# Expert weights of a mixture of experts in 4 MB fetches from the ninth expert, one loop from the first expert, and another first gather

## The chip, the cores and the metric

The kernel runs on one core of one Trainium2 chip. The metric is the device time of one execution in microseconds (us), as the median of three runs. A difference under about 0.2% (2.3 us) can hardly be told from none here.

## The reference, cut to what matters

A one-layer encoder step for 256 prompt tokens and 32 sample tokens, 1024 wide: a LayerNorm, one input projection, sparse attention with an indexer, causal pooling, an output projection, a LayerNorm, then a mixture of experts and a last LayerNorm. The mixture takes most of the time. In it every token is sent to 4 of 32 experts, and each expert has 12 MB of float32 weights:

```python
for e in range(N_EXPERTS):                       # 32 experts
    gu = xt @ w1[e] + b1[e]                      # (288, 1024) @ (1024, 2048)
    gate = jnp.minimum(gu[:, :D_FF], SWIGLU_LIMIT)
    up = jnp.clip(gu[:, D_FF:], -SWIGLU_LIMIT, SWIGLU_LIMIT)
    act = (up + 1) * (gate * jax.nn.sigmoid(SWIGLU_ALPHA * gate))
    out = out + gates[:, e:e + 1] * (act @ w2[e] + b2[e])    # (288, 1024) @ (1024, 1024)
```

## The kernel before, in words

Everything up to the router is done once, in program order. Then the experts follow one after the other, and all their weights have to be read from HBM once, 403 MB.

**Weights.** `ring` in SBUF has six slots of 2 MB, so it holds exactly one expert: slots 0 to 3 are quarters of w1, slots 4 and 5 the halves of w2. Expert 0 is fetched during the stages before. After that SP fetches slot s of expert e as soon as TensorE has freed slot s of expert e - 1 (`load`, lines 455 to 459; the semaphore is `slot_free[s]`). Every partition receives 16 KB in one piece per fetch. The landing raises `w_in_slot[s]`, on which TensorE waits before it uses the slot. The last half of w2 of the last expert comes in four fetches of 512 KB, each with its own semaphore (line 471).

**One expert on TensorE** (`expert`, line 903). An expert works on a block of 64 of its tokens. (A second block for an expert with more than 64 tokens is a loop of its own, `more > 0`; with these inputs it never runs, and TensorE jumps over its code.) The steps are: the bias (line 836), 32 float32 matmuls of 512 columns for w1 (`up_products`, line 845; each is two instructions in the trace, so 64 of them, 16 for each slot), `combine` of the expert before (line 890), `gather_rows` for the next expert (line 819, needs `pick`, which VectorE makes at line 1477), the turn of the hidden values (`turn_h`, line 854), the two halves of w2 (`down_products`, line 870), and between them the transposes of the gathered rows (`turn_x`, line 828). `turn_pick` (lines 880 and 883) turns the next expert's selection matrix. The 64 tokens fill half of the array's columns, so two matmuls (g = 0, 1), for the two halves of 512 output columns, run side by side.

**The first expert.** Its tokens are gathered in another way, since the rows aren't split into bf16 parts yet: line 792 multiplies pieces of `rows`, as the stationary operand, with the selection matrix `pick0`; the 32 sample rows follow at line 806 once their selection is known, and VectorE adds the two (line 1509). After this addition VectorE makes the gates (lines 1511 to 1523, `gate_split`), the starting values of the accumulators, and splits `rows` in three bf16 parts in four instructions over all three tiles (lines 1532 to 1535, `split_ready`). Only then does it come to `pick` of expert 1.

**The order of the code.** `expert(0)` and `expert(1)` are written out, a loop runs from 2 to 30, and `expert(31, last=True)` is written out again. Each of them starts with the test for more tokens and the code of the second block.

**The tail.** After the last w2 product TensorE adds the last expert's contribution to the sums of tiles 0, 2 and 1, in this order (`start_sum`, `add_last`, lines 984 and 992). ScalarE and VectorE normalise them: ScalarE starts with tile 2's sum (line 1213), then takes the root for tile 0 (line 1006), on which VectorE's `centre(0)` waits (line 1615) before `centre(1)` begins (line 1607). GpSimd has one addition at the end.

```python
def load(e, s):
    src = w1_part(col(e), s) if s < 4 else w2_v[col(e), s - 4]
    sp.wait_ge(slot_free[s], e)
    sp.dma_start(ring[:, s, :], src.rearrange("e p n -> p (e n)")).then_inc(w_in_slot[s], 16)
```

## Time and profile before

| | |
|---|---|
| median of 3 runs | 1136.07 us (1135.74 to 1136.48) |
| the profiled execution's own time | 1135.52 us |
| its span in the trace | 1133.7 us |
| TensorE matmul busy | 1058.4 us, 93% |
| VectorE, ScalarE, GpSimd busy | 397.8, 195.4, 15.4 us |
| read from HBM | 420.11 MB |
| chain that ended last | DMA 50%, TensorE 40%, VectorE 8% |
| fetches of 2 MB into `ring` | 191, median 22.0 us from issue to landing |

The span is cut into 40 slices of 28.3 us in the page of the profile. Up to the seventh the data rate is below 330 GB/s, from the ninth to the thirty-eighth it is 427 to 430 GB/s. Busy shares are averages: both TensorE and the DMA engines look full, and which of them sets the time has to be read from what waits for what in each stretch.

### The profile page before, as it was taken

To read this page: it belongs to the slowest core of one execution; us is meant where nothing else is said; L and a number is where in the kernel's file an instruction comes from. 1 tells how busy PE (TensorE), PEld (TensorE's weight loads), DVE (VectorE), ACT (ScalarE), POOL (GpSimd) and SP (SyncE) were. 2 spreads that over 40 slices of the span, in tenths; PEclk is the share of its full clock that TensorE was granted. 3 is DMA by queue.
4 is the path that set the end of the run, shared out by engine and by line. 5 is a ranking of instruction groups with operands and counts; after the bars stand their busy time and mean duration, and the time that the engine had idled before them with its cause. 6 is when DMAs were issued, how large, how long until landed. Compare 5 with 4: busy or idle time off the path is not lost.

```text
span 1133.7 us, 13776 instructions
## 1 busy us (share of the span) xinstructions
PE 1058.4 (93%) x5318; PEld 438.3 (39%) x5319; DVE 397.8 (35%) x682; ACT 195.4 (17%) x439; POOL 15.4 (1%) x26
## 2 busy tenths in 40 slices
PE   8989999999999999999999999999999999999986
PEld 7765465333333333333333333333333333333331
DVE  7682357322333332222222222222222222222215
ACT  3334110111111111111111111111111111111113
POOL 1003000000000000000000000000000000000000
PEclk9999897999999999999999999999999999999988
DMA  9750333999999999999999999999999999999991
GB/s 324 265 223 1 126 136 156 380 427 427 429 430 427 429 430 427 429 429 428 429 429 428 429 428 428 429 428 428 429 428 429 429 427 430 429 427 430 429 380 42
DMA packets 37633, 421.91 MB, mean 372 GB/s; under 512 B 6333, under 2 KB 6973, under 8 KB 13066
## 3 DMA queue, kind: packets, MB, share of 16 engines
q1 hardware_dynamic: 37418, 420.93, 88.5%
q10 hardware_dynamic: 192, 0.66, 0.2%
q8 instruction: 16, 0.26, 0.1%
q14 instruction: 7, 0.06, 0.0%
HBM read 420.11 MB, written 1.46 MB: 372 GB/s over the span
## 4 chain that ended last, share of the span: by engine, by line
DMA 50%; PE 40%; DVE 8%; issue 1%; ACT 1%; DVEq 0%; SPq 0%; ACTq 0%
DMA ring<-in_w_dram 49%; PE ps L845 18%; PE ps L870 6%; PE ps L576 4%; PE ps L693 3%; PE ps L890 1%; DVE area L1563 1%; PE ps L555 1%; PE ps L792 1%; DVE area L1554 1%; DVE area L1557 1%; DVE area L1550 1%; PE ps L640 1%; PE ps L828 1%; DVE area L1551 1%
## 5 line engine op out<-in xcount | busy, mean ns | idle before, releaser
L845 PE MATMUL ps<-ring,area 128*64 128x512 f32 x2048 | 453.7, 597 | 26.6 <-DMA ring<-in_w_dram 26.6
L845 PEld LDWEIGHTS ps<-ring,area 128*64 128x64 f32 x2048 | 142.5, 138 | 320.4 <-issue 254.6
L870 PE MATMUL ps<-ring,area 128*64 128x512 f32 x1024 | 231.9, 595 | 0.0
L1550 DVE TENSOR_SCALAR area<-ps 128x512 f32<-128x512 f32 x32 | 22.1, 691 | 382.3 <-PE ps L845 382.3
L1563 DVE TENSOR_TENSOR area<-area,ps 128x1024 f32<-128x1024 f32 (+1 forms) x96 | 116.4, 1214 | 51.9 <-PE ps L890 51.9
L870 PEld LDWEIGHTS ps<-ring,area 128*64 128x64 f32 x1024 | 69.7, 136 | 124.8 <-issue 122.3
L1177 ACT ACTIVATE area<-area 128x512 f32<-128x512 f32 x32 | 20.1, 630 | 492.8 <-DVE area L1550 492.8
L1542 DVE SCALAR_TENSOR_TENSOR y_sb<-ps,gcol,y_sb 64x512 fp32r<-64x512 f32 x62 | 46.5, 751 | 98.4 <-ACT y_sb L1149 98.0
L890 PE MATMUL ps<-y_sb,giveT 128*128 128x512 f32 x192 | 69.4, 443 | 11.9 <-DVE area L1563 11.9
L819 PE MATMUL ps<-area 128*64 128x512 bf16 x558 | 66.1, 382 | 2.2 <-DVE area L1477 2.2
L1149 ACT ACTIVATE y_sb<-ps,gcol 64x512 fp32r<-64x512 f32 x62 | 42.4, 683 | 92.4 <-PE ps L870 91.7
L576 PE MATMUL ps<-tokT,area 128*128 128x288 f32 (+1 forms) x224 | 56.8, 414 | 0.0
L576 PEld LDWEIGHTS ps<-tokT,area 128*128 128x128 f32 (+1 forms) x224 | 42.2, 190 | 13.5 <-issue 0.9
L890 PEld LDWEIGHTS ps<-y_sb,giveT 128*128 128x128 f32 x192 | 29.1, 191 | 43.1 <-issue 25.1
L1196 ACT COPY area<-ps 128x512 f32<-128x512 f32 x31 | 18.2, 587 | 154.4 <-PE ps L828 154.4
L819 PEld LDWEIGHTS ps<-area 128*64 128x64 bf16 x558 | 28.9, 109 | 35.9 <-issue 11.0
L1483 DVE CAST sel<-same_exp 96x64 bf16 (+1 forms) x32 | 6.1, 192 | 82.3 <-PE ps L870 82.3
L854 PE MATMUL ps<-ident,area 128*128 128x128 f32 x128 | 23.8, 309 | 8.3 <-DVE area L1557 8.3
L828 PEld LDWEIGHTS ps<-ident,tokT 128*128 128x128 f32 x124 | 17.3, 209 | 25.2 <-issue 25.2
L854 PEld LDWEIGHTS ps<-ident,area 128*128 128x128 f32 x128 | 17.8, 208 | 23.6 <-DVE area L1557 21.3
L836 PE MATMUL ps<-area,sel 96*64 96x512 bf16 x128 | 20.8, 406 | 5.5 <-issue 4.6
L1477 DVE TENSOR_TENSOR area<-iota_slot,kv_rows 128x384 bf16<-128x384 f32 (+2 forms) x33 | 18.0, 546 | 22.2 <-issue 22.1
(231 smaller groups left out, 627.0 us busy)
## 6 DMA issues: line engine op xcount, KB each, us to landing
ring<-in_w_dram SPq DMA_DIRECT2D x191, 2048.0 KB, 22.0
area<-in_w_o_dram SPq DMA_DIRECT2D x1, 4096.0 KB, 13.4
area<-in_w_in_dram SPq DMA_DIRECT2D x1, 2560.0 KB, 16.2
area<-in_w_in_dram SPq DMA_DIRECT2D x1, 2336.0 KB, 9.2
area<-in_w_in_dram SPq DMA_DIRECT2D x1, 2048.0 KB, 20.4
ring<-in_w_dram SPq DMA_DIRECT2D x4, 512.0 KB, 19.8
lnb<-in_ln_g_dram SPq DMA_DIRECT2D x3, 512.0 KB, 10.4
lnb<-in_ln_b_dram SPq DMA_DIRECT2D x3, 512.0 KB, 11.7
```

The lines of the kernel that those rows point to most:

```text
L576: last = mm(ps[0:w, proj_bank(i), 0:TOK], w_in_sb[chunk][:, j, c0:c0 + w], tokT[:, j, :], start=(j == 0), stop=(j == KT - 1))
L693: last = mm(dst, mixed[:, k, t0:t0 + n], w_o_sb[:, k, half * 512:(half + 1) * 512], start=(start and k == ks[0]), stop=(stop and k == ks[-1]))
L819: last = mm(ps[g * BLK:(g + 1) * BLK, 2, :], one[:, t, 0, :], rows_b[:, t, part, g * 512:(g + 1) * 512], start=(t == 0 and part == 0), sto ...
L828: last = tr(ps[:, 2, c * P:(c + 1) * P], gx[:, c:512:4], ident[:, :])
L845: last = mm(ps_gu[g * BLK:(g + 1) * BLK, c, :], x[:, spot(k), :], w[:, a:a + 512], start=False, stop=(k == KT - 1))
L854: last = tr(dst[:, c * P:(c + 1) * P], h_sb[:, c:512:4], ident[:, :])
L870: last = mm(ps_y[g * BLK:(g + 1) * BLK, :], hT[:, c, h, :], w2_t[:, h, c, g * 512:(g + 1) * 512], start=False, stop=(h == 1 and c == 3))
L890: last = mm(dst[:, g, :], giveT[:, t * P:(t + 1) * P], y_sb[:, g * 512:(g + 1) * 512], start=True, stop=True)
L1149: nc.scalar.activation(y_sb[0:BLK, g * 512:(g + 1) * 512], ps_y[r, :], ACT.Copy, scale=gcol[r, :]).then_inc(done, 1)
L1542: ins = v.scalar_tensor_tensor(y_sb[BLK:P, g * 512:(g + 1) * 512], ps_y[r, :], gcol[r, :], y_sb[0:BLK, g * 512:(g + 1) * 512].bitcast(F32) ...
L1550: v.tensor_scalar(g_sb, ps_gu[:, 0, :], LIMIT, None, ALU.min).then_inc(gate, 1)
L1563: v.tensor_tensor(acc, acc, src[0:n, :, :], ALU.add).then_inc(done, 1)
```

## The change

1. **Fetches.** Experts 1 to 8 are fetched as before, now in a loop. From expert 9 (`FIRST_WIDE`) to expert 30 SP fetches pairs of slots, 4 MB each with 32 KB in one piece for every partition (`load_pair`), and waits for both slots of a pair to be free. Expert 31 is fetched by slots of 2 MB, the last one too.
2. **The signal.** A pair raises only `w_in_slot[s]`. GpSimd waits for it and raises `w_in_slot[s + 1]`.
3. **Layout.** For w2 to lie in 32 KB pieces, partition p now holds rows 8p to 8p + 7. So that the hidden values come out in that order, the w1 product reads its moving operand in groups of 4 columns, every other group (`half_of`): g = 0 takes columns 0 to 3, 8 to 11, ..., g = 1 the others. The bias is read in the same way.
4. **First gather.** `pick0` is now the stationary operand and `rows` the moving one: six matmuls of 512 columns, then a copy by ScalarE, `turn_x`, and a copy to `xT`. The addition on VectorE is gone. `turn_pick` for expert 0, with its wait for `gate_split`, moves ahead of the first w1 product.
5. **Split.** The split of `rows` is done tile by tile, in 12 instructions instead of 4.
6. **Loop.** The loop runs from expert 0 to 30, and the test for more tokens of the next expert (`more_tokens(e + 1)`) stands at its end.
7. **Tail.** The last sums are made in the order of tiles 0, 1, 2.

```diff
-        w2_v = w2[0].rearrange("e (h p c) n -> e h p (c n)", h=2, c=4)
+        w2_v = w2[0].rearrange("e (p h c) n -> e h p (c n)", h=2, c=4)
+        w2_whole = w2[0].rearrange("e (p q) n -> e p (q n)", q=KT)
@@ SP
+            def load_pair(e, s):
+
+                src = w1_v[col(e), s // 2] if s < 4 else w2_whole[col(e)]
+                sp.wait_ge(slot_free[s], e)
+                sp.wait_ge(slot_free[s + 1], e)
+                sp.dma_start(ring[:, s:s + 2, :], src.rearrange("e p n -> p (e n)")).then_inc(w_in_slot[s], 16)
+
+            with sp.Fori(1, FIRST_WIDE) as e:
                 for s in range(NSLOT):
                     load(e, s)
-            for s in range(NSLOT - 1):
+            with sp.Fori(FIRST_WIDE, NE - 1) as e:
+                for s in range(0, NSLOT, 2):
+                    load_pair(e, s)
+            for s in range(NSLOT):
                 load(NE - 1, s)
-            sp.wait_ge(slot_free[5], NE - 1)
-            for c in range(4):
-                sp.dma_start(w2_t[:, 1, c, :], w2_v[NE - 1, 1, :, c * D:(c + 1) * D]).then_inc(tail_in[c], 16)
@@ GpSimd
+            with pool.Fori(FIRST_WIDE, NE - 1) as e:
+                for s in range(0, NSLOT, 2):
+                    pool.wait_ge(w_in_slot[s], 16 * (e + 1))
+                    pool.sem_inc(w_in_slot[s + 1], 16)
@@ TensorE
+            def gather_first(t, stop):
+
+                for g in range(2):
+                    last = mm(ps[g * BLK:(g + 1) * BLK, 2, :], pick0[:, t, 0, :], rows[:, t, g * 512:(g + 1) * 512],
+                              start=(t == 0), stop=stop)
+                return last
...
+            keep_warm(4)
             pe.wait_ge(pick_ready, 1)
+            gather_first(2, True).then_inc(x_first, 1)
...
+            def half_of(w, c, g):
+
+                return w[:, c * F:(c + 1) * F].rearrange("p (m g q) -> p m g q", g=2, q=4)[:, :, g, :]
...
-                            last = mm(ps_gu[g * BLK:(g + 1) * BLK, c, :], x[:, spot(k), :], w[:, a:a + 512],
+                            last = mm(ps_gu[g * BLK:(g + 1) * BLK, c, :], x[:, spot(k), :], half_of(w, c, g),
...
+            keep_warm(4)
+            turn_x(x_first_sb, 1, x_gathered)
+            pe.wait_ge(gate_split, 1)
+            turn_pick(pick, ps_g, slice(0, 1), giveT_done)
...
-                    for t in (2, 1):
+                    for t in (1, 2):
...
-            expert(0)
-            expert(1)
-            with pe.Fori(2, NE - 1) as e:
+            more_tokens(0)
+            with pe.Fori(0, NE - 1) as e:
                 expert(e)
+                more_tokens(e + 1)
@@ VectorE
-            dve.wait_ge(x_first_sb, 1)
-            dve.wait_ge(x_gathered, 1)
-            v.tensor_tensor(xT, xT, ps[:, 3, :].rearrange("p (k s) -> p k s", k=KT), ALU.add).then_inc(xT_ready, 1)
...
+            dve.wait_ge(x_gathered, 1)
+            for t in range(NT):
+                link(v.tensor_copy(rows_b[:, t, 0, :], rows[:, t, :]))
...
```

SyncE's queue, its loop of fetches. Before, six fetches of a slot (128x4096 float32, 2 MB) for an expert:

```order
L459 ISA [waits slot_free0]
L459 DMA ring<-in_w_dram 128x4096
L459 ISA [waits slot_free1]
L459 DMA ring<-in_w_dram 128x4096
L459 ISA [waits slot_free2]
L459 DMA ring<-in_w_dram 128x4096
```

With the change, from expert 9 to 30:

```order
L467 ISA [waits slot_free1,slot_free0]
L467 DMA ring<-in_w_dram 128x8192
L467 ISA [waits slot_free3,slot_free2]
L467 DMA ring<-in_w_dram 128x8192
L467 ISA [waits slot_free5,slot_free4]
L467 DMA ring<-in_w_dram 128x8192
```

Half as many fetches stand in the queue, each twice as large and behind two waits.

TensorE's stream at the last expert. Before, between the end of the loop (L976) and the last expert's bias (L836) stood the code of the second block:

```order
L976 COMPARE_AND_BRANCH
L904 TENSOR_LOAD blocks_i
L904 ISA x2
L905 COMPARE_AND_BRANCH
L906 TENSOR_LOAD blocks_i
L906 ISA x2
L907 UNCONDITIONAL_BRANCH
L812 ISA
L819 MATMUL ps<-area,tokT 64x512 x18
```

With the change that code is inside the loop, and the last expert's products (L847, L855) follow right behind the loop's end (L989):

```order
L920 COMPARE_AND_BRANCH
L918 UNCONDITIONAL_BRANCH
L989 REGISTER_ALU
L989 COMPARE_AND_BRANCH
L847 MATMUL ps<-area,sel 64x512 x4
L855 MATMUL ps<-ring,area 64x512 x32
L897 MATMUL ps<-y_sb,giveT 128x512 x4
```

So the jump over the second block's code is no longer the last thing between the loop and the last expert.

TensorE's stream before the first expert. Before, the gather (L792, L806: sixteen and eight matmuls of 64 columns) ran up to the test for more tokens:

```order
L792 MATMUL ps<-area,rows 128x64 x8
L555 MATMUL ps<-ident 128x128 x2
L806 MATMUL ps<-area,rows 128x64 x8
L904 TENSOR_LOAD blocks_i
L904 ISA x2
L905 COMPARE_AND_BRANCH
```

With the change:

```order
L565 MATMUL ps<-ident 128x128 x4
L803 MATMUL ps<-rows,area 64x512 x2
L565 MATMUL ps<-ident 128x128 x4
L836 MATMUL ps<-ident,tokT 128x128 x4
L887 MATMUL ps<-ident_b,area 128x128 x3
L890 MATMUL ps<-gate_b,area 128x3 x3
L917 TENSOR_LOAD blocks_i
```

The gather is shorter, and the transposes (L836) and `turn_pick` (L887, L890) now stand between it and the test.

## Rows read from the trace of the kernel before

**Rows 1.** Stretches: from:to, us, busy us (x) PE PEld DVE ACT POOL, clock, DMA, GB/s

```profile
198.00:227.00 29.00, 25.87 (x136) 9.71 (x138) 10.49 (x13) 4.34 (x9) 0.00 (x0) 1.00 0.93 381
312.00:600.00 288.00, 275.44 (x1408) 99.81 (x1408) 85.66 (x112) 43.78 (x91) 0.00 (x0) 1.00 1.01 428
1086.00:1092.00 6.00, 5.18 (x16) 1.88 (x18) 0.00 (x0) 0.00 (x0) 0.00 (x0) 0.50 1.02 429
```

**Rows 2.** Chain that ended last: start us, us, what

```profile
423.40 24.82 DMA ring<-in_w_dram
...
1035.57 3.68 PE ps L845 x16
1039.41 25.47 DMA ring<-in_w_dram
```

**Rows 3.** Timeline before the first expert's products: start us, us, engine, line, operation, idle

```profile
180.07 0.69 DVE L1509 TENSOR_TENSOR area<-area,ps 128x512 f32<-128x512 f32 x1 [5.87 <-PE ps L806]
180.81 1.06 PE L836 MATMUL ps<-area,sel 96*64 96x512 bf16 x4 [0.85 <-DVE area L1509]
183.15 0.27 DVE L1523 TENSOR_TENSOR gate_b<-kv_rows,gate_b 128x99 bf16<-128x99 f32 x1
```

**Rows 4.** DMA queues, PE's code queue q8, in 175:182 and in 1082:1104

```profile
q8 instruction: 2, 0.03, 1.8%
...
q8 instruction: 2, 0.03, 0.6%
```

**Rows 5.** Timeline, first expert's turn from up to down products

```profile
197.24 0.70 PE L890 MATMUL ps<-y_sb,giveT 128*128 128x512 f32 x2
200.16 2.13 PE L819 MATMUL ps<-area 128*64 128x512 bf16 x18 [2.22 <-DVE area L1477]
204.91 3.60 PE L870 MATMUL ps<-ring,area 128*64 128x512 f32 x16
```

**Rows 6.** DMA packets and data queue, 66:74 (w_o, 4 KB runs), then 250:1080

```profile
DMA packets 807, 3.31 MB, mean 414 GB/s; under 512 B 0, under 2 KB 0, under 8 KB 806
q1 hardware_dynamic: 806, 3.30, 101.1%
...
DMA packets 24420, 355.60 MB, mean 428 GB/s; under 512 B 2716, under 2 KB 2716, under 8 KB 2716
q1 hardware_dynamic: 24419, 355.59, 100.6%
```

**Rows 7.** Timeline of TensorE, experts 29 and 30, then the last

```profile
1039.15 0.73 PE L890 MATMUL ps<-y_sb,giveT 128*128 128x512 f32 x2
1053.22 10.47 PE L845 MATMUL ps<-ring,area 128*64 128x512 f32 x48
1064.93 3.65 PE L845 MATMUL ps<-ring,area 128*64 128x512 f32 x16 [1.24 <-DMA ring<-in_w_dram]
...
1086.82 1.06 PE L836 MATMUL ps<-area,sel 96*64 96x512 bf16 x4 [4.63 <-issue]
1087.65 16.37 PE L845 MATMUL ps<-ring,area 128*64 128x512 f32 x64
```

**Rows 8.** Table load of ScalarE at line 1177: duration min/median/max ns, start

```profile
L1177 ACT ACT_TABLE_LOAD  x1: 1283/1283/1283, 176.4 to 176.4; - x1
```

**Rows 9.** Weight loads: min/median/max ns, first and last start us

```profile
L792 PEld LDWEIGHTS ps<-area,rows x32: 308/329/331, 167.4 to 174.9; 128*128 128x128 f32 x32
...
L762 PEld LDWEIGHTS ps<-w_router_sb,tokT x48: 106/192/192, 157.5 to 166.6; 128*128 128x128 f32 x32, 128*32 128x32 f32 x16
```

**Rows 10.** Timeline of the tail: last sums and what follows

```profile
1120.42 1.05 PE L992 MATMUL ps<-tokT 64*32 64x512 f32 x4
1121.52 1.01 ACT L1213 ACTIVATE area<-ps 32x1024 f32<-32x1024 f32 x1 [5.04 <-PE ps L992]
1122.98 0.16 DVE L1615 RECIPROCAL rstd<-std 128x1 f32<-128x1 f32 x1 [1.28 <-ACT std L1006]
1124.49 1.30 DVE L1607 BATCH_NORM_STATS2 stats<-ps 128x6 f32<-128x512 f32 x2 [1.35 <-PE ps L992]
```

More of the change, by code:

```diff
@@ L309, in encoder_kernel @@
         acc_done = [sem(f"acc_done{t}") for t in range(NT)]
-        tail_in = [sem(f"tail_in{c}") for c in range(4)]
         last_give = sem("last_give")
@@ L789, in _ @@
             pe.wait_ge(pick_first, 1)
[L790 to L803 removed]
+            def gather_first(t, stop):
[3 more added lines that the diff above has]
+                return last
+            gather_first(0, False)
+            gather_first(1, False)
+            pe.wait_ge(gates_ready, 2)
+            for u in range(NT):
+                mm(ps[:, 5, 0:NE], before[:, :] if u == 2 else ones_b[:, :], chosen_b[:, u, :],
+                   start=(u == 0), stop=(u == 2))
+            for u in range(NT):
+                total = mm(ps[:, 5, NE:2 * NE], ones_b[:, :], chosen_b[:, u, :],
+                           start=(u == 0), stop=(u == 2))
+            total.then_inc(prefix_ps, 1)
+            keep_warm(4)
             pe.wait_ge(pick_ready, 1)
[L805 to L808 removed]
+            gather_first(2, True).then_inc(x_first, 1)
             def gather_rows(one, ready, want, done, e):
                 pe.wait_ge(ready, want)
[L813 to L815 removed]
                 for t in range(NT):
@@ L927, in expert @@
                             pe.wait_ge(x_acc_done[t], b + 1)
+            def expert(e, last=False):
                 pe.wait_ge(xT_ready, e + 1)
@@ L952, in expert @@
                     return
-                if isinstance(e, int) and e == 0:
-                    pe.wait_ge(gate_split, 1)
-                    turn_pick(pick, ps_g, slice(0, 1), giveT_done)
                 pe.wait_ge(y_ready, e + 1)
@@ L1152, in _, with more_tokens @@
             act.wait_ge(x_first, 1)
-            copy(xT, ps_x).then_inc(x_first_sb, 1)
+            copy(gx, ps[:, 2, :]).then_inc(x_first_sb, 1)
+            act.wait_ge(x_gathered, 1)
+            copy(xT, ps_x).then_inc(xT_ready, 1)
             act.wait_ge(blocks_ready, 1)
-            def expert(e, last=False):
+            def more_tokens(e):
                 more = act.value_load(blocks_i[0:1, 0, col(e)], min_val=0, max_val=LAST_BLK - 1)
@@ L1175, in expert @@
                         nc.scalar.activation(x_y, ps_y, ACT.Copy, scale=x_gcol[:, :]).then_inc(x_y_ready, 1)
+            def expert(e, last=False):
                 act.wait_ge(gate_ready, e + 1)
@@ L1204, in expert @@
                 gated_high(y_high)
-            expert(0)
-            expert(1)
-            with act.Fori(2, NE - 1) as e:
+            more_tokens(0)
+            with act.Fori(0, NE - 1) as e:
                 expert(e)
+                more_tokens(e + 1)
             expert(NE - 1, last=True)
@@ L1565, in _, with more_tokens @@
             dve.wait_ge(blocks_ready, 1)
-            def expert(e, last=False):
+            def more_tokens(e):
                 more = dve.value_load(blocks_i[0:1, 0, col(e)], min_val=0, max_val=LAST_BLK - 1)
@@ L1576, in expert @@
                             accumulate(t, x_comb_done[t], b + 1, x_acc_done[t])
+            def expert(e, last=False):
                 if not last:
@@ L1581, in expert @@
                 if last:
-                    for t in (0, 2, 1):
+                    for t in range(NT):
                         accumulate(t, comb_done[t], NE, acc_done[t], src=ps_sum[t])
@@ L1593, in expert @@
                 gated_low(e)
-            expert(0)
-            expert(1)
-            with dve.Fori(2, NE - 1) as e:
+            more_tokens(0)
+            with dve.Fori(0, NE - 1) as e:
                 expert(e)
+                more_tokens(e + 1)
             expert(NE - 1, last=True)
```

45 lines of the change are left out of this document (9 added, 36 removed).

## The prediction

> **What bounds the kernel now.** I read the stretches first, then the chain of waits, then the timeline at the places where the chain changes hands. In the stretches the reader is to see that from the middle of the first experts on the DMA engines are full, at 428 GB/s, while TensorE is busy 275 of 288 us [rows 1]: both look like the bound. The chain decides it. From 423 us on its pieces are a fetch of 25 us and 3.7 us of TensorE, over and over [rows 2]; TensorE waits at the last slot of w1 in each expert, and one period is 1064.93 - 1035.57 = 29.36 us [rows 2, 7]. A slot is 2.10 MB, at 428 GB/s 4.9 us, so a fetch that lands after 25 us has spent 20 of them behind others: the queue of transfers is the bound, not the latency of one. TensorE alone would need 14.07 us from the end of the w1 products to the next ones (1039.15 to 1053.22 [rows 7]) and 64 x 0.218 = 14.0 us for these (48 instructions in 10.47 us [rows 7]), some 28.0 us. So the end of the kernel is the time at which the stream of refills starts, plus 31 experts' transfers, plus what TensorE does after it has lost touch with the stream at the end.
>
> That last part is not short. The last expert's bias starts only after 4.63 us in which TensorE waits for nothing the profile shows, and its w1 products take 16.37 us, for 14.0 elsewhere [rows 7]; the granted clock is 0.50, the 1.2 GHz level, in the stretch behind that idle time [rows 1]. Two packets of 16 KB on TensorE's code queue fall in this stretch [rows 4], while of 24420 packets in 250 to 1080 us all but one are data [rows 6]: I read the 4.63 us as code that had to be fetched, since it stands beyond the loop and beyond the jump over the second block. The last weights are there before they are needed, so the four small fetches at the end hide nothing.
>
> **The change, part by part**, each against the profiled execution's own 1135.52 us, which is 0.55 us under the median.
>
> *Larger packets.* The fetch of w_o in 4 KB packets shows 1.011 x 16 engines x 8 us / 806 = 160.5 ns a packet; in the long stretch, without the 2716 signals, it is 1.006 x 16 x 830 / 21704 = 615.5 ns for 16 KB [rows 6]. A line through the two has 8.8 ns fixed and 37.0 ns per KB of 1000 bytes. A 32 KB packet then takes 1222 instead of 1231 ns, 0.71% less. What counts is the transfers from expert 9 to w1 of expert 30, 21.7 x 29.36 = 636 us: a gain of 4.5 us. Bounds: 0, if the engines cut the run into 16 KB anyway or the difference isn't fixed; 9, if the fixed part is twice my two-point value.
> By the Trainium skill (DMA: Bandwidth & Descriptors, Why small descriptors are slow) a packet has a fixed overhead of about 3 cycles; at the 850 MHz that the same page gives for the fabric this is 3.5 ns where the trace has 8.8, and an estimate by that page would be a gain of 1.8 us instead of 4.5, the whole sum 2.7 us higher.
>
> *Pairs.* SP now waits for two slots. When slot 3 of expert 9 was asked for, at 423.40 us, it landed 24.82 us later [rows 2], with 4.9 of its own: some 18 us of other transfers stood ahead. Waiting for the second slot costs 16 x 0.218 = 3.5 us in w1, and somewhat more in w2, so from expert 9 on the queue never runs dry: 0. GpSimd's forwarding is needed only 3.5 us after the landing, and GpSimd has nothing else to do: 0. But TensorE gets slots 2 and 3 at one time and has 7.1 us to do after the landing instead of 3.65. Its cycle from landing to landing becomes 7.1 + 14.07 + 7.0 = 28.2 us, still under 29.1, so nothing is lost in the loop; at the end, where TensorE alone sets the pace, it is 3.5 us later.
>
> *The last expert's code.* It now stands directly behind the loop's end, which has been run 30 times, so the first part needs no fetch and the next can come during 14.0 us of products. I take the 4.63 us away, and with them the slow clock. TensorE would start these products 7.1 + 14.07 = 21.2 us after the landing in expert 30 (before: 1087.65 - 1064.93 = 22.7), and need 14.0 instead of 16.4: 35.2 instead of 39.1, with the pairs 3.9 us earlier. The last slot of w1 lands 29.4 us after that landing and is needed 31.6 after, so no wait comes back. Bounds: 7.0 worse if the code is still fetched.
>
> *Tail order.* Before, ScalarE began with tile 2 at 1121.52, VectorE had tile 0's root at 1122.98, and `centre(1)` started at 1124.49 with its sum [rows 10]. Now tile 2 comes last, when tile 1 did, at about 1124.45. ScalarE starts 3.0 us later, the root is ready 1.46 + 0.2 us after that, and `centre(1)` starts at 1126.2: 1.7 us lost. Nothing covers it. The four small fetches go at no cost, since the slot has landed well before the w2 product.
>
> *Start.* The old gather's weight loads go by 0.24 us each (32 in 7.5 us [rows 9]), 48 in all; the six new matmuls cost 0.43 us each. VectorE, which sat idle 5.87 us before the addition [rows 3], goes on at once; its gate work (180.76 to 183.42 [rows 3]) ends at 174.2 - 2.0 + 2.7 = 174.9 us, the 2.0 because the counts' matmuls come after four short instead of sixteen slow instructions. TensorE turns `pick` until 175.5. Then comes the jump over the second block. Two code packets lie in 175 to 182 us [rows 4]: this jump misses as the last expert's did. With 4.6 us for it the products start at 180.2 instead of 180.8 [rows 3]: -0.5 us. Bounds: -5.3 if the code is there, +1.0 if the fetch is a bit slower than that.
>
> *First turn.* Between the w1 and w2 products of expert 0 TensorE waited 2.22 us for `pick`, and went from 197.24 to 204.91 [rows 5]. VectorE is now 8.5 us earlier with the gates, far more than the 12 instructions in place of 4 can add. The w2 product starts about 3 us earlier, and the refill of slot 4 with it. In this stretch the stream carried 381 instead of 428 GB/s, 3.2 us lost in 29 [rows 1]; I give 2.0 back, bounds 0 and 3.2.
>
> *The strided read.* 0, with the rival below. *The table load* in ScalarE's loop, 1.28 us [rows 8], lies in the 14.0 us of products in which ScalarE has nothing to do; if it came later it would delay the sigmoid by as much, inside TensorE's 1 us of slack. *The loop from 0* and the register arithmetic: 0, the matmul queue covers them.
>
> Sum: -4.5 - 3.9 + 1.7 - 0.5 - 2.0 = -9.2 us, 1126.3 for the profiled execution, **1126.8** on the scale of the median.
>
> **Rivals.**
> *A, the strided read makes TensorE the bound (slower).* For it: where a weight load reads one float of every four (line 792) it takes 329 ns, where it reads in a row (line 762) 192 [rows 9], 137 ns for 128 columns. The new moving read skips a group of four after each group, 128 times per instruction. If a skip costs what a lone float did, it is 0.137 us for each of 32 side-by-side pairs, 4.4 us per expert. The cycle is then 28.0 + 4.4 = 32.4, over 29.36, and 30 of them take 972 us where 906 pass now from the first bias to the last (180.81 to 1086.82 [rows 3, 7]); with 2.0 for the last products and 1.7 for the tail that is 1136.1 + 69.7 = 1206 us. It decides from 0.26 of this price on (28.2 + 1.16 = 29.36). Against it: groups of four floats are not single ones.
> On this the Trainium skill (SBUF — State Buffer, Specifications (TRN2)) says that lines are 16 bytes and that only reads with fewer than two hits in a line lose bandwidth. Four floats fill a line, and by that rule A doesn't happen; the two weight loads agree with it.
> *B, no larger packets.* The transfers are cut as before: -4.7, 1131.4. For it: no packet over 16 KB is in the trace. Against it: every run up to 16 KB came as one packet [rows 6].
> *C, the last expert's code is fetched all the same.* +7.0: -2.2, 1133.9. B and C together: +2.3, 1138.4.
> *D, the first jump finds its code,* or the stream starts earlier for another reason: -14.0, 1122.1.
>
> **How the numbers follow.** Forecast 0.38, B 0.20, C 0.16, B and C 0.07, D 0.10, A 0.09. Faster by over 0.2% (2.3 us, about what a measurement can tell): forecast, B, D and the better part of C, 0.06: 0.74. Within it: the rest of C and half of B with C: 0.13. Slower: A and the rest: 0.13. The range runs from just under D, 1121.5, to just over B with C, 1139; A is left out.
>
> **What would show it.** Data packets of 32 KB and over 430 GB/s from 420 us on; a period of 29.1 us with TensorE waiting at slot 2 for about 1 us, not at slots 2 and 3; no idle time of 4 us before the last bias and 14.0 us for the last w1 products; `centre(1)` 1.7 us later behind the last w2 product than before; no wait of line 827 for `pick` in expert 0. Wrong is the forecast if 48 instructions of line 855 in a row take more than 10.5 us, if the rate stays at 428, or if SP's queue of fetches runs empty after expert 9.

## The result, and the profile after

| | before | after |
|---|---|---|
| median | 1136.07 us | 1128.09 us (1127.28 to 1129.7) |
| ratio to before, 95% interval | | 0.9921 [0.9908, 0.9934] |
| the profiled execution's own time | 1135.52 us | 1127.28 us |
| its span | 1133.7 us | 1125.5 us |
| ScalarE busy | 195.4 us | 234.3 us (31 table loads, 39.8 us) |

The change makes the kernel 0.8% faster, 8.0 us by the medians and 8.2 us by the two profiled executions. The forecast was 1126.8 us, in a range from 1121.5 to 1139.

The stretches after (from:to, us, busy us (x) of PE PEld DVE ACT POOL, clock, DMA, GB/s), for [rows 1]:

```profile
198.00:227.00 29.00, 28.44 (x154) 10.66 (x152) 9.42 (x13) 5.93 (x11) 0.00 (x0) 1.00 1.00 425
312.00:600.00 288.00, 275.42 (x1397) 100.31 (x1397) 83.72 (x110) 55.54 (x99) 0.00 (x0) 0.99 1.01 431
```

Behind the first expert the stream of weights carries 425 instead of 381 GB/s, from expert 9 on 432 instead of 428 (431 over the second stretch, which begins before that). The chain that ended last, for [rows 2]:

```profile
1027.79 7.11 PE ps L855 x32
1035.10 21.79 DMA ring<-in_w_dram
1056.93 7.11 PE ps L855 x32
1078.21 13.76 PE ps L855 x64
```

It is still a fetch and TensorE in turn, with 7.1 us of products behind each landing instead of 3.7, and one period is 1056.93 - 1027.79 = 29.14 us (29.36 before). Behind expert 30 no fetch stands in it. TensorE's timeline from the first turn and from the end, for [rows 5, 7] (start us, us, engine, line, operation, idle time before it):

```profile
180.37 16.55 PE L855 MATMUL ps<-ring,area 128*64 128x512 f32 x64
...
197.51 2.13 PE L827 MATMUL ps<-area 128*64 128x512 bf16 x18
...
201.86 3.60 PE L877 MATMUL ps<-ring,area 128*64 128x512 f32 x16
...
1056.93 7.09 PE L855 MATMUL ps<-ring,area 128*64 128x512 f32 x32 [0.99 <-DMA ring<-in_w_dram]
...
1077.57 0.64 PE L847 MATMUL ps<-area,sel 96*64 96x512 bf16 x4
1078.04 13.90 PE L855 MATMUL ps<-ring,area 128*64 128x512 f32 x64
1091.88 1.20 PE L897 MATMUL ps<-y_sb,giveT 128*128 128x512 f32 x4
1094.96 0.72 PE L864 MATMUL ps<-ident,area 128*128 128x128 f32 x4 [1.88 <-DVE area L1577]
...
1096.59 8.73 PE L877 MATMUL ps<-ring,area 128*64 128x512 f32 x32
```

The first products of the kernel before, beside the first of these lines:

```profile
181.67 15.38 PE L845 MATMUL ps<-ring,area 128*64 128x512 f32 x64
```

They now start 1.30 us earlier but take 1.17 us longer. Three things are gone: the wait for `pick` in expert 0, the 4.63 us ahead of the last bias, and the slow last w1 products (13.90 instead of 16.37 us). One thing is new: the last w2 products. Their 32 instructions ran from 1108.66 to 1115.62 us before, in 6.96 us; now they take 8.66 (the next instruction of TensorE, the first sum, starts at 1105.25). The granted clock, the third number from the end in these stretches, says why:

```profile
1093.00:1096.60 3.60, 1.51 (x11) 0.95 (x12) 3.22 (x5) 3.06 (x7) 0.00 (x0) 1.00 0.28 114
1096.70:1100.00 3.30, 3.30 (x12) 0.81 (x10) 1.82 (x2) 0.00 (x0) 0.00 (x0) 0.50 0.00 0
```

The clock was at 0.50, the 1.2 GHz level, for some 3.4 us. Ahead of that TensorE had worked 1.51 of 3.6 us, since it waited 1.88 us for the gated hidden values.

Cut at the points where the chain changes hands, the 8.2 us lie as follows:

| stretch (us) | before | after | change | forecast |
|---|---|---|---|---|
| from the start to the first refill asked for | 186.79 | 186.80 | 0.0 | -0.5 |
| from there to the landing of slot 3 (with 2) in expert 9 | 261.43 | 258.13 | -3.3 | -2.0 |
| from there to the same in expert 30 | 616.71 | 612.00 | -4.7 | -4.5 |
| landing to the end of the last w1 products | 39.02 | 34.95 | -4.1 | -3.9 |
| the turn between w1 and w2 | 4.71 | 4.71 | 0.0 | 0 |
| last w2 products | 6.96 | 8.66 | +1.7 | 0 |
| from there to the end of the span | 18.08 | 20.25 | +2.2 | +1.7 |
| sum | | | -8.2 | -9.2 |

The landings are at 423.40 + 24.82 = 448.22 and at 1064.93 us before [rows 2, 7], and at 444.93 and 1056.93 us after.

### The profile page after: what moved, and what is told of

Its sections match the earlier page's. It is cut to its first block, busy times and chain, and to the rows that moved or that the text cites. A ratio compares the mean times of both kernels' runs of the same rounds, so it can differ in the third digit from the quotient of the medians.

```text
span 1125.5 us, 13844 instructions
## 1 busy us (share of the span) xinstructions
PE 1054.6 (94%) x5298; PEld 437.2 (39%) x5299; DVE 395.4 (35%) x689; ACT 234.3 (21%) x470; POOL 15.4 (1%) x26
## 4 chain that ended last, share of the span: by engine, by line
PE 49%; DMA 41%; DVE 7%; issue 1%; ACT 1%; SPq 0%; DVEq 0%; ACTq 0%
DMA ring<-in_w_dram 41%; PE ps L855 27%; PE ps L877 7%; PE ps L586 4%; PE ps L703 3%; PE ps L897 1%; DVE area L1583 1%; PE ps L565 1%; DVE area L1574 1%; DVE area L1577 1%; DVE area L1570 1%; PE ps L847 1%; PE ps L836 1%; DVE area L1571 1%; PE ps L650 1%
## 5 line engine op out<-in xcount | busy, mean ns | idle before, releaser
L855 PE MATMUL ps<-ring,area 128*64 128x512 f32 x2048 | 453.7, 597 | 22.9 <-DMA ring<-in_w_dram 22.9
L855 PEld LDWEIGHTS ps<-ring,area 128*64 128x64 f32 x2048 | 149.7, 138 | 309.6 <-issue 257.3
L877 PEld LDWEIGHTS ps<-ring,area 128*64 128x64 f32 x1024 | 70.1, 137 | 126.1 <-issue 123.7
L1198 ACT ACT_TABLE_LOAD x31 | 39.8, 1283 | 1.0 <-issue 0.5
L836 PEld LDWEIGHTS ps<-ident,tokT 128*128 128x128 f32 x128 | 17.8, 209 | 25.2 <-issue 25.2
L1213 ACT COPY tokT<-ps 128x512 f32<-128x512 f32 x31 | 18.1, 585 | 42.4 <-PE ps L827 42.4
```

The lines of the kernel that those rows point to most:

```text
L855: last = mm(ps_gu[g * BLK:(g + 1) * BLK, c, :], x[:, spot(k), :], half_of(w, c, g), start=False, stop=(k == KT - 1))
L877: last = mm(ps_y[g * BLK:(g + 1) * BLK, :], hT[:, c, h, :], w2_t[:, h, c, g * 512:(g + 1) * 512], start=False, stop=(h == 1 and c == 3))
L1198: nc.scalar.activation(sig_sb, g_sb, ACT.Sigmoid, scale=SWIGLU_ALPHA).then_inc(sig_ready, 1)
```

## The experiments

Each group was compared with the kernel before on its own chip: 1137.30 us for no pairs, pairs of 16 KB runs, the old order of the last sums and the small matmuls; 1136.13 for the code moved, the code put back, the late pick and no first test; 1136.97 for the two shifts, one float of four and the combined version. The start of the program differs between executions by up to 3.0 us (the first refill goes out at 186.6 to 189.6 us in kernels with the same start), which is as much as some of the effects; where a profile shows the stretch, the stretch decides.

### Packets and pairs

**No pairs.** All fetches by slots, as in `with sp.Fori(1, NE - 1)`, and no loop on GpSimd:

```diff
-            with sp.Fori(1, FIRST_WIDE) as e:
+            with sp.Fori(1, NE - 1) as e:
                 for s in range(NSLOT):
                     load(e, s)
-            with sp.Fori(FIRST_WIDE, NE - 1) as e:
-                for s in range(0, NSLOT, 2):
-                    load_pair(e, s)
```

> The changed kernel with every fetch one slot of 2 MB in 16 KB packets, no pairs, no forwarding on GpSimd. If the 32 KB packets raised the rate, the period goes back from 29.14 to 29.36 us (21.7 of them: +4.7), but TensorE gets the slots one by one, which brings the last expert's products up to 3.5 us closer to the landing in expert 30, less 1.2 us that they then wait for their last slot of w1: in sum 1130.5 us. If the packets did nothing and the better rate has another cause, it is 1125.8 us: the period stays and the phase of the pairs is won back.

Measured: 1128.57 us, ratio 0.9925 [0.9911, 0.9938].

**Pairs of 16 KB runs.**

```diff
+        w1_quarters = w1[0].rearrange("e (h a p c) n -> e h p a (c n)", h=2, a=2, c=2)
+        w2_halves = w2[0].rearrange("e (a p c) n -> e p a (c n)", a=2, c=4)
-                src = w1_v[col(e), s // 2] if s < 4 else w2_whole[col(e)]
+                src = w1_quarters[col(e), s // 2] if s < 4 else w2_halves[col(e)]
...
-                sp.dma_start(ring[:, s:s + 2, :], src.rearrange("e p n -> p (e n)")).then_inc(w_in_slot[s], 16)
+                sp.dma_start(ring[:, s:s + 2, :], src.rearrange("e p a n -> p (e a) n")).then_inc(w_in_slot[s], 16)
```

> The pairs of 4 MB stay, with the same waits, signals and number of fetches, but each partition gets them in two runs of 16 KB from two places of the row range (the rows of w1 and w2 then lie in other partitions than the products assume, so the output is another; the amount of work is the same). If the packet's size is what counts, the packets take 615 ns each and the period is 29.36 us: 21.7 x 0.22 = +4.7, 1132.8 us. If it is that a fetch is larger, or that there are fewer signals, it stays at 1128.1 us.

Measured: 1132.90 us, ratio 0.9957 [0.9943, 0.9970]. The packets of 430 to 1050 us: first the changed kernel, then this one (count and rate, then the data queue with packets, MB and share of 16 engines):

```profile
DMA packets 9194, 267.72 MB, mean 432 GB/s; under 512 B 1024, under 2 KB 1024, under 8 KB 1024
q1 hardware_dynamic: 9194, 267.72, 100.3%
```

```profile
DMA packets 17221, 265.64 MB, mean 428 GB/s; under 512 B 1008, under 2 KB 1008, under 8 KB 1008
q1 hardware_dynamic: 17221, 265.64, 100.6%
```

The same 4 MB fetches, waits and signals with 16 KB runs are back at 428 GB/s. Their period, from the timeline:

```profile
1034.89 7.09 PE L856 MATMUL ps<-ring,area 128*64 128x512 f32 x32 [1.22 <-DMA ring<-in_w_dram]
...
1064.25 7.09 PE L856 MATMUL ps<-ring,area 128*64 128x512 f32 x32 [1.22 <-DMA ring<-in_w_dram]
```

It is 29.36 us. So it is the packet's size that counts, and neither the size of a fetch nor the number of signals. The kernel without pairs has the same period, 1091.15 - 1061.80 = 29.35 us:

```profile
1061.80 3.65 PE L847 MATMUL ps<-ring,area 128*64 128x512 f32 x16 [1.22 <-DMA ring<-in_w_dram]
...
1091.15 3.65 PE L847 MATMUL ps<-ring,area 128*64 128x512 f32 x16 [1.20 <-DMA ring<-in_w_dram]
1094.73 1.20 PE L889 MATMUL ps<-y_sb,giveT 128*128 128x512 f32 x4
```

Its landing in expert 30 is 4.9 us later than in the changed kernel, and from it to the end of the last w1 products pass 1094.73 - 1061.80 = 32.9 us instead of 34.95: the pairs cost 2.0 us at the end, with the 1.2 us wait for the last slot that I had expected. That it came out at 1128.6 and not at 1130.5 us has one more cause: its clock does not fall in the last w2 products (7.03 us), which saves 1.7. So the larger packets with their pairs bring 2.9 us where the clock stays up, and in this pair of kernels the clock gives most of that back.

### The last expert's code

**The kernel before with the code moved**, on TensorE alone:

```diff
-            def expert(e, last=False):
+            def more_tokens(e):
...
...
+            def expert(e, last=False):
                 pe.wait_ge(xT_ready, e + 1)
...
+            more_tokens(0)
             expert(0)
+            more_tokens(1)
             expert(1)
+            more_tokens(2)
             with pe.Fori(2, NE - 1) as e:
                 expert(e)
+                more_tokens(e + 1)
```

> The kernel before, with one edit on TensorE alone: the test for more tokens and the second block's code stand at the end of an expert instead of at its head, so the last expert's products follow right behind the loop. If the 4.63 us and the slow clock behind them are code that has to be fetched, they go: the last up products end 31.7 us after the landing in expert 30, plus 1.2 us that they then wait for their last slot, where it was 39.0: 6.1 us less, 1130.0 us (1131.7 if the clock then falls in the last w2 products, as in the changed kernel). If they come from the register reads of the test, which stay, it is 1136.1 us.

Measured: 1133.36 us, ratio 0.9974 [0.9965, 0.9983]. At the last expert the idle time and the slow clock are gone:

```profile
1068.06 3.65 PE L845 MATMUL ps<-ring,area 128*64 128x512 f32 x16 [1.23 <-DMA ring<-in_w_dram]
...
1085.26 0.62 PE L836 MATMUL ps<-area,sel 96*64 96x512 bf16 x4
...
1097.43 3.65 PE L845 MATMUL ps<-ring,area 128*64 128x512 f32 x16 [1.25 <-DMA ring<-in_w_dram]
```

From the landing to the end of the w1 products it takes 32.9 instead of 39.0 us, the 6.1 that I had worked out. The test's register reads are still there, so they were not the cause. But only half of it reaches the result. Most of the rest went at the start of expert 3:

```profile
274.58 1.06 PE L836 MATMUL ps<-area,sel 96*64 96x512 bf16 x4 [4.88 <-issue]
```

The idle time has moved: 4.88 us of it, with the clock at 0.50 behind it, and the landing in expert 30 is 3.1 us later than in the kernel before [rows 7], 0.5 of it from a later start (the first refill goes out at 187.32 us). 3.1 - 6.1 = -3.0 us, which is 1133.1.

**The code put back in the changed kernel.**

```diff
-            more_tokens(0)
             with pe.Fori(0, NE - 1) as e:
+                more_tokens(e)
                 expert(e)
-                more_tokens(e + 1)
+            more_tokens(NE - 1)
```

> The changed kernel with the opposite edit on TensorE alone: the test and the second block's code stand at the head of the loop and once more between the loop and the last expert. Code theory: the idle time of 4 to 5 us and the half clock come back before and in the last w1 products: +7.0, less 1.7 if the clock then does not fall in the w2 products: 1133.4 to 1135.1 us. Rival, that pairs or larger packets shortened this stretch: 1128.1 us.

Measured: 1128.29 us, ratio 0.9930 [0.9917, 0.9943]. TensorE at the last expert, and its code queue between 1076 and 1092 us:

```profile
1078.67 0.64 PE L847 MATMUL ps<-area,sel 96*64 96x512 bf16 x4
```

```profile
q8 instruction: 1, 0.02, 0.4%
```

This was a clear miss. The second block's code stands between the loop and the last expert again, TensorE jumps over it, and there is no idle time. One code packet comes in these 16 us (two in the kernel before, none in the changed one), but TensorE doesn't wait for it: it starts at 1080.7 us, while the products run. In each of the four idle times of 4.6 to 5.5 us of this document a packet on the code queue starts 1.7 to 2.4 us after TensorE has stopped (at 1084.1 us in the kernel before, where TensorE stops at 1082.2), and TensorE goes on 1.6 to 2.2 us after it has ended. So code that must be fetched is still the best reading of the 4.63 us, though no run takes the packet away alone. But "behind a jump" isn't the condition. A new theory: it depends on where in memory the loop's end and the last expert lie, relative to the pieces in which code is fetched. Two kernels tried it, with nothing else changed than the number of small matmuls at the very start, where TensorE waits for its input.

```diff
             pe.wait_ge(ident_ready, 1)
-            keep_warm(12)
+            keep_warm(20)
```

> The kernel before with eight small matmuls more at its very start, where TensorE waits anyway: nothing else than that all of its later code lies a little further on. The run with the code put back showed no idle time at the last expert though the jump was there, so what counts may be where the loop and the last expert lie against the pieces in which code is fetched. If the shift brings the loop's end and the last expert's code to such a place, the 4.63 us and the slow clock go as in the run with the code moved: 1133.4 us or, with the 6.1 us worked out there, 1130.0. If what counts is the order of the code alone, it stays at 1136.1 us.

Measured: 1132.87 us, ratio 0.9965 [0.9953, 0.9977]. TensorE:

```profile
1066.76 3.65 PE L845 MATMUL ps<-ring,area 128*64 128x512 f32 x16 [1.24 <-DMA ring<-in_w_dram]
...
1083.96 0.62 PE L836 MATMUL ps<-area,sel 96*64 96x512 bf16 x4
```

Eight matmuls more at the start of the old kernel, and the 4.63 us at its end are gone; from the landing to the end of the w1 products it takes 32.9 us, as with the code moved. So the order of the code alone doesn't make the idle time. (1.6 of the 6.1 us went again since here the clock falls at the last w2 products: 8.34 us instead of 6.96, and 0.2 in the turn before them. Another 1.8 went because the landing in expert 30 is later, 1.0 of it from a later start of the refills.) The shift also made a new idle time of 1.84 us, and not right at a jump: TensorE stops in the middle of the w1 products of expert 2, 2.3 us after it began that expert's bias. A code packet starts at 243.9 us, 0.7 before the stop.

```profile
246.43 12.61 PE L845 MATMUL ps<-ring,area 128*64 128x512 f32 x57 [1.84 <-issue]
```

The other one, with `keep_warm(4)` in the kernel with the code put back:

> The run with the code put back (second block ahead of the last expert), with eight small matmuls fewer at the very start: its code lies a little nearer. If the place against the pieces of code counts, the idle time of 4 to 5 us before the last bias and the half clock behind it come back: 1133.4 to 1135.1 us. If the order of the code or the loop from expert 0 is what counts, no idle time and 1128.3 us.

Measured: 1125.58 us, ratio 0.9893 [0.9877, 0.9909]. No idle time came back at the last expert, so the condition stays unknown, and this one shift neither shows nor refutes that the place in memory counts: three kernels that have the jump there (this one and the two before it) don't wait, and the kernel before does. The shift worked at another place, at the first jump:

```profile
179.13 0.66 PE L847 MATMUL ps<-area,sel 96*64 96x512 bf16 x4 [1.42 <-issue]
```

Here TensorE waits 1.42 us. The same kernel without the shift, and then the changed kernel:

```profile
181.11 1.06 PE L847 MATMUL ps<-area,sel 96*64 96x512 bf16 x4 [4.61 <-issue]
```

```profile
177.19 0.39 PE L847 MATMUL ps<-area,sel 96*64 96x512 bf16 x1 [1.32 <-issue]
179.93 1.06 PE L847 MATMUL ps<-area,sel 96*64 96x512 bf16 x3 [2.35 <-issue]
```

The intervals of the two kernels with the code put back are apart: 0.9930 against 0.9893, some 3 us for eight small matmuls. In the profiles the first refill goes out at 187.73 us without the shift and at 185.10 with it.

### The start and the first turn

**No first test.** `more_tokens(0)` left out on TensorE: a second block of expert 0 wouldn't be computed.

> The changed kernel without the test for more tokens and the second block of expert 0 on TensorE (with these inputs it never runs): no jump stands ahead of the first products. If the 1.32 and 2.35 us of idle time around the first bias are the jump's missing code, the first w1 products start at 177.6 instead of 180.4 us and the whole stream 2.8 us earlier: 1125.3 us. If the code has to be fetched whether there is a jump or not, 1128.1 us.

Measured: 1126.02 us, ratio 0.9905 [0.9891, 0.9919].

```profile
175.98 13.93 PE L855 MATMUL ps<-ring,area 128*64 128x512 f32 x64
...
209.17 1.07 PE L847 MATMUL ps<-area,sel 96*64 96x512 bf16 x4 [5.53 <-issue]
```

The first idle time goes, and with it the slow clock that made the first 64 products take 16.55 us in the changed kernel: the first refill goes out at 179.80 us, 7.0 earlier. But the first jump is now the one at the end of expert 0, and it costs 5.53 us with the clock at 0.50 behind it. In 198 to 227 us the stream carries 325 GB/s, and most of the lead is lost: the landing in expert 30 is at 1056.48 us, 0.45 earlier, and the profiled execution is 0.5 us faster. That the idle time goes with the first jump holds for this pair of kernels and is no rule: with the code moved it came at expert 3, behind several jumps.

**A late pick.** In the changed kernel, on VectorE:

```diff
+                for _ in range(8 if t == 2 else 0):
+                    link(v.tensor_tensor(rows_b[:, t, 2, :], rows[:, t, :], rows_b[:, t, 1, :], ALU.subtract))
                 v.tensor_tensor(rows_b[:, t, 2, :], rows[:, t, :], rows_b[:, t, 1, :], ALU.subtract).then_inc(split_ready, 1)
```

> The changed kernel with eight repeats of the last instruction of the split on VectorE (1.23 us each, 9.8 in all), so that pick of expert 1 is ready at 200.3 us as before and not at 190.5. If the first turn is where 3.3 us of the stream came from, TensorE waits 2.2 us again between the w1 and w2 products of expert 0, the stretch of 29 us behind it carries some 380 instead of 428 GB/s, and the time is 1131.2 us. If the stream would have caught up anyway (the queue refills later), it is 1128.1 us.

Measured: 1130.73 us, ratio 0.9952 [0.9939, 0.9965].

```profile
200.56 2.13 PE L827 MATMUL ps<-area 128*64 128x512 bf16 x18 [3.05 <-DVE area L1498]
...
1060.46 7.09 PE L855 MATMUL ps<-ring,area 128*64 128x512 f32 x32 [0.99 <-DMA ring<-in_w_dram]
```

TensorE waits 3.05 us. Its first w2 product starts at 205.31 us, 3.45 later than in the changed kernel, and 860 us later the landing in expert 30 is 1060.46 - 1056.93 = 3.5 us later: nothing in between made up for it. This shows what an early `pick` is worth; which part of the change makes it early, the new gather or the split tile by tile, no run tells apart.

### The tail and the clock

**The old order of the last sums:** `(2, 1)` again on TensorE and `(0, 2, 1)` on VectorE.

> The changed kernel with the old order of the last sums (tiles 0, 2, 1) on TensorE and VectorE. My theory: the sum of tile 1 on VectorE starts 1.55 us earlier behind the last w2 product (8.87 instead of 10.42 us), and the end comes as much earlier: 1126.5 us. The rival, that the last store sets the end whatever the order: within 0.3 us of 1128.1.

Measured: 1126.56 us, ratio 0.9900 [0.9885, 0.9916]. The tail from the first of the last sums on, and the last two stores, of this kernel and of the changed one:

```profile
1107.99 1.98 PE L998 MATMUL ps<-area,ident 128*128 128x512 f32 x4
...
1116.86 1.30 DVE L1632 BATCH_NORM_STATS2 stats<-ps 128x6 f32<-128x512 f32 x2 [1.34 <-PE ps L1006]
...
1122.49 0.34 SPq L478 DMA_DIRECT2D out_dram<-area  x1
1123.67 0.35 ACTq L1256 DMA_DIRECT2D out_dram<-area  x1
```

```profile
1105.25 1.98 PE L998 MATMUL ps<-area,ident 128*128 128x512 f32 x4
...
1115.67 1.28 DVE L1632 BATCH_NORM_STATS2 stats<-ps 128x6 f32<-128x512 f32 x2
...
1121.28 0.34 SPq L478 DMA_DIRECT2D out_dram<-area  x1
1122.46 0.35 ACTq L1256 DMA_DIRECT2D out_dram<-area  x1
```

`centre(1)` starts 8.87 us behind the first sum in the old order and 10.42 in the new one. From there on the two run alike up to the last store, but this takes 2.4 us to the end of the span (1126.1) in the old order and 3.0 (1125.5) in the new one. In all 18.1 against 20.25 us: the new order costs 2.1.

**Eight small matmuls in the last expert's idle time.**

```diff
                     combine(2, comb_done[2], dst=ps_sum[2])
+                    keep_warm(8, bank=4)
                     pe.wait_ge(last_give, 1)
```

> The changed kernel with eight extra small matmuls in the last expert, where TensorE waits some 1.9 us for the gated hidden values (between combine and turn_h). If the idle time there is why the granted clock falls to half for 3.4 us of w2 products, the w2 products take 6.96 instead of 8.66 us and the time is 1126.4 us. If the clock falls for another reason (a dip comes after a certain stretch of load), it stays at 1128.1 us or is up to 0.3 us worse by the added matmuls.

Measured: 1127.16 us, ratio 0.9907 [0.9892, 0.9922].

```profile
1095.55 1.95 PE L565 MATMUL ps<-ident 128*128 128x128 f32 x16
...
1099.24 7.03 PE L877 MATMUL ps<-ring,area 128*64 128x512 f32 x32
```

The w2 products take 7.0 us and the clock stays at its higher level. That speaks for the idle time as the cause, but doesn't settle it. Of the eleven profiled kernels without these matmuls and without the 4.63 us, the clock fell in the last w2 products in eight and stayed up in three (no pairs, pairs of 16 KB runs, the code moved in the kernel before); with them it stayed up in both kernels that have them, which at three in eleven would happen by chance once in some 13 times.

### The strided read

The moving operand of the bias and the w1 products with one float of every four:

```diff
-                return w[:, c * F:(c + 1) * F].rearrange("p (m g q) -> p m g q", g=2, q=4)[:, :, g, :]
+                return w[:, 2 * c + g:2 * F:4]
```

> The changed kernel with the moving operand of the bias and w1 products read one float of every four (over the whole row of 2048 floats) instead of in groups of four; every weight is used once, but in another column, so the output is another. If a lone float costs a moving read what it cost the weight load (137 ns for 128 columns, so 0.55 us for 512), a pair of products takes some 1.5 us instead of 0.44 and TensorE sets the pace: 16 pairs of two halves, +17 us for each expert, some 1600 us. If a moving read of float32 has room for it, 0.218 us for each instruction stays and the time is 1128 us.

Measured: 1591.85 us, in a single run. The w1 products in the groups of both kernels (count, busy us, mean ns of one, idle time before), the changed kernel first:

```profile
L855 PE MATMUL ps<-ring,area 128*64 128x512 f32 x2048 | 453.7, 597 | 22.9 <-DMA ring<-in_w_dram 22.9
```

```profile
L855 PE MATMUL ps<-ring,area 128*64 128x512 f32 x2048 | 928.2, 1079 | 0.0
```

TensorE never waits for weights here and sets the pace. 474.5 us more for 1024 pairs of instructions is 463 ns a pair, 0.90 ns a column, beside the 1.07 (137 ns for 128) of the weight load in [rows 9]. So the price was real, and it is the group of four that avoids it: in the changed kernel an instruction takes 597 ns on average, as it did before. In the last w2 products of this kernel the clock fell too:

```profile
1561.50 8.40 PE L877 MATMUL ps<-ring,area 128*64 128x512 f32 x32
```

### A version that beats both

The changed kernel with the old tail order, the small matmuls in the last expert, and w1 of expert 30 by single slots (this part is shown; GpSimd's forwarding follows it):

```diff
-            with sp.Fori(FIRST_WIDE, NE - 1) as e:
+            with sp.Fori(FIRST_WIDE, NE - 2) as e:
                 for s in range(0, NSLOT, 2):
                     load_pair(e, s)
+            for s in range(4):
+                load(NE - 2, s)
+            load_pair(NE - 2, 4)
...
```

> The changed kernel with three edits: the old tail order (tiles 0, 2, 1), eight small matmuls in the last expert's idle time, and w1 of expert 30 by single slots. From the runs so far: the tail 2.1 us shorter (18.11 instead of 20.25 us from the last w2 product to the end), the w2 products 1.7 us, and of the 3.4 us between 7.09 and 3.65 us of products behind the landing in expert 30 some 1.0 go to a wait for the last slot of w1, so 2.4: 1128.1 - 6.2 = 1121.9 us. If the landing in expert 30 comes later by single slots than by the pair (their requests wait for the same transfers), the third part is 0: 1124.3 us.

Measured: 1123.00 us, ratio 0.9873 [0.9855, 0.9891], the lowest median of all (its interval overlaps those of the old order of the last sums and of the kernel with the code put back and shifted, but not that of the changed kernel). The w2 products take 7.0 us and the tail 18.1, as expected. The third part was worth less:

```profile
1030.27 7.09 PE L860 MATMUL ps<-ring,area 128*64 128x512 f32 x32 [0.99 <-DMA ring<-in_w_dram]
...
1051.38 13.90 PE L860 MATMUL ps<-ring,area 128*64 128x512 f32 x64
...
1079.31 13.90 PE L860 MATMUL ps<-ring,area 128*64 128x512 f32 x64
```

TensorE doesn't wait at all in experts 30 and 31: the last pair, in expert 29, has put it 7.1 us behind a landing, and 27.93 us for an expert is only 1.2 us under the stream's 29.14. So what single slots win is 1.2 us for each expert that has them, up to the 2.0 that the pairs cost, and not 2.4 at once. 1121.9 + 1.2 = 1123.1.

## Why the prediction was right, point by point

- **Larger packets, -4.5.** Measured -4.7. The packets come whole, and 267.72 MB in 9194 - 1024 = 8170 data packets are 32.8 KB each. Their price follows best from the periods: the 12 MB of an expert are 48 packets of 16 KB for each of the 16 engines, 29.36 / 48 = 611.7 ns a packet, or 24 of 32 KB, 29.14 / 24 = 1214.2 ns. Twice 611.7 less 1214.2 is a fixed part of 9.2 ns, within a nanosecond or so, and my line through 4 and 16 KB had 8.8. (The shares of the rows give 1.003 x 16 x 620 / 8170 = 1218 and 1.006 x 16 x 620 / 16213 = 615.5 ns, so 13 ns. But with shares above 100% the times of packets overlap, and 13 ns would have meant a gain of 6.8 us.) The Trainium skill (DMA: Bandwidth & Descriptors, Why small descriptors are slow) with its 3 cycles, an estimate of 3.5 ns, is too low for this kernel; the estimate of 1.8 us worked out from it would have missed most of this term. Rival B (no larger packets) is refuted.
- **Pairs, 0 in the loop and +3.5 at the end.** In the loop it holds: TensorE waits 0.99 us for the second pair of w1 in each expert, and the data rate shows no gap. (My "some 18 us" of transfers ahead of slot 3 should have been 24.82 - 4.9 = 19.9; nothing hangs on it.) At the end the pairs cost 2.0 in the comparison with single slots, since these would have waited 1.2 us for their last slot; inside my term of 3.9 this was counted rightly, since I had 35.2 us for that stretch and 34.95 were measured.
- **The last expert's code, -3.9 with the pairs.** The size was right, -4.1. The reason was half wrong. "It stands beyond the loop and beyond the jump over the second block" is not what makes the idle time: with the code put back it stays away, and with the old order and eight small matmuls more at the start it goes as well. Most likely the change took the 4.63 us away by shifting the code, but which shifts do it is not shown, and my step held by luck as far as the order goes. Rival C (the code is fetched all the same) had a chance of 0.16; after these runs I would call such an idle time unpredictable from the diff.
- **Tail order, +1.7.** Measured +2.2 in the two traces and 2.1 by the old order put back. The delay of `centre(1)` was 1.55; the 0.6 us that I had left out lies behind the last store.
- **Start, -0.5.** Measured 0.0. `gate_split` came at 175.15 + 0.27 us, near the 174.9 I had worked out, and TensorE stood idle at the jump, as expected (1.32 + 2.35 us around the first bias instead of my 4.6), with the first product at 180.37. But my 180.8 for the kernel before was the start of the bias; its products started at 181.67. So TensorE gained 1.3 us up to here and not 0.5, and lost 1.2 in the products: the clock at the 1.2 GHz level, which ended at about 184.6 us before, now lasts until 185.3. Rival D (the first jump finds its code) did not come; the run without the first test shows that it can't be had by leaving out one jump, the shifted kernel with the code put back that some of it can (its first refill goes out 1.7 us earlier than in the changed kernel).
- **First turn, -2.0.** This term was too small: -3.3. I counted what the stretch behind it had lost in rate; the run with the late pick shows that the whole delay stays in the result (3.45 us at the first w2 product, 3.5 at the landing in expert 30). In the changed kernel this product starts 204.91 - 201.86 = 3.05 us earlier, the "about 3 us" that I had worked out, and I gave back only 2.0 of it.
- **The last w2 products, 0.** This was not in the sum, and it cost 1.7 us: the clock. With the start and the tail, 0.5 us each, it is 2.7 us too much; the first turn gave 1.3 more than forecast and the packets and the last expert 0.2 each. So the profiled execution is only 1.0 us above my 1126.3: the terms are close, but that the total is this close is partly luck, since their errors cancel.
- **Strided read, 0, and rival A.** The products take 597 ns on average, as in the kernel before. Rival A priced a skip at what a lone float costs; the run with one float of four shows that this price exists (1592 us) and that groups of four don't pay it. The rule of the Trainium skill (SBUF — State Buffer, Specifications (TRN2)), that a read needs at least two hits in a line of 16 bytes for full bandwidth, agrees with both.
- **Table load, GpSimd's forwarding, four small fetches, 0.** ScalarE is busy 39 us more and nothing on the chain moved by it; the turn between w1 and w2 takes 4.71 us in both. TensorE runs the 32 products of a pair without a wait for the forwarded slot. The rest left no trace in any stretch.

What stays open: what makes TensorE wait at the last expert (the place of the code in memory was only argued), and why the clock fell in the last w2 products in eight kernels and not in three others with the same idle time.

## What to carry to other kernels

Cut two traces at the points where the chain changes hands and give each stretch its own term; changes of a few microseconds can then be read although whole times differ by as much between chips. Where the stream of fetches is the bound, a refill that is asked for late at the start stays late until the end (3.45 us were still 3.5 after 860 us here), and a larger piece per landing costs its own processing time once, where TensorE loses touch with the stream. Idle time of TensorE that nothing releases, next to packets on its code queue, can come and go with eight unrelated matmuls: before crediting a change with it, shift the code alone and look again.

## What the runs showed of the hardware that I had not expected

- An idle time of 4.6 to 5.5 us at a jump, with code packets beside it, moved with small shifts of the code: 4.63 us at the last expert before, 4.88 at expert 3 with the code moved, 5.53 at expert 1 without the first test, and 4.61 or 1.42 at the first bias with eight small matmuls more or fewer ahead. Each of the long ones was followed by the granted clock at 0.50. With eight small matmuls more in the kernel before, 1.84 us of idle time came in the middle of the 64 w1 products of expert 2.
- The granted clock fell for some 3.4 us behind a stretch in which TensorE had worked 1.51 of 3.6 us, which cost 1.7 us of w2 products. It also fell once in the middle of the changed kernel, from 444.7 to 448.1 us, behind 2.63 us of waiting at expert 9, and 32 w1 products took 8.64 us instead of 7.09. That cost nothing: the next 21 landings take 612.00 us, and 1058.04 - 446.02 = 612.02 us in the kernel with the code put back, whose clock stays up there.
- A moving operand of single floats, 16 bytes apart, costs 0.90 ns more a column for a pair of side-by-side float32 products; groups of four floats with gaps of four cost nothing.
- The end of the span came 0.6 us later behind the last store when the second of the three was asked for 0.77 us behind the first (1120.51 and 1121.28) than when it came 2.2 us behind (1120.27 and 1122.49): the first was still moving.
